# 128 unused bytes per partition ahead of the activation buffers of a two-block transformer kernel

## The chip, the cores and the metric

The kernel runs on one core of a Trainium2 chip. The metric is the device time of one execution in microseconds (us); three executions were timed and their median is taken.

## The reference, cut to what matters

Two transformer blocks are applied to 256 tokens of width 2048, all in float32. The first has forgetting attention and dilated attention, and an expert layer (PEER) whose 16,384 experts are computed densely here and gated; the second has sliding-window attention with sinks, gated linear attention and stick-breaking attention, and a squared-ReLU feed-forward layer. Almost all of the arithmetic is in the matrix products:

```python
proj = xn @ w_in[layer]                 # 2048 x 6160, later 2048 x 5136
h = h + mixed @ w_out[layer]            # 2048 x 2048
q = (xt @ w_query)                      # 2048 x 2048
u = jnp.take(expert_down, ec, axis=0)   # experts: 16384 x 2048 down, 16384 x 2048 up
...
jnp.square(jax.nn.relu(h @ w1)) @ w2    # 2048 x 8192 and 8192 x 2048
```

## The kernel before

**The product.** Every weight matrix is streamed through SBUF once, in chunks of 256 rows by 512 columns (440 columns in the first input projection, "in1", and 428 in the second, "in2"). SyncE's queue loads a chunk into one of four slots of `raw` (line 420). ScalarE makes a rounded float32r copy `w_hi` (line 585) and VectorE the remainder `w_lo = raw - w_hi` (line 590). The activations are kept transposed, split in the same way: `x_hi` and `x_lo` hold the input of a layer, `a_hi` and `a_lo` the hidden values, each 16 x 256 float32r columns, 16,384 bytes, in each of 128 partitions.

A chunk is two row tiles of 128 (`kk`), for two tiles of 128 tokens (`t`), in three products, hence twelve matmuls:

```python
wh = w_hi[:, c % RING, kk * n:kk * n + n]
wl = w_lo[:, c % RING, kk * n:kk * n + n]
xh, xl = hi[:, k, t * P:t * P + P], lo[:, k, t * P:t * P + P]
mm(o, xh, wh, start=(k == 0), stop=False)
mm(o, xh, wl, start=False, stop=False)
last = mm(o, xl, wh, start=False, stop=(k == KT - 1))
```

The first operand of `mm` behind the output, a tile of activations, is the stationary one: a LDWEIGHTS (engine PEld in the profile) reads 128 columns of it, which are 512 bytes of each partition, and the MATMUL then streams the 512, 440 or 428 columns of weights. The lines are 1674 to 1676 in `chunk` (expert layer and feed-forward layer) and 1831 to 1833 in `part` (everything else). Every matmul has a LDWEIGHTS of its own.

**The order.** TensorE's instructions are written out in one order, with `Fori` loops over the like rounds of the expert and feed-forward layers. Between the chunks stand the small matmuls of the attention, and transposes: `pe.transpose(out, in_, ident)` loads `in_` as the stationary operand and streams the identity from `fix`. The transposes that the prediction speaks of are those of the spilled hidden values (`hid_ring`, line 1950), of the residual `h` and of `mix` (line 2016); the sums of the gates of the linear attention (line 2051) load 96 columns of `g_log` and stream 2 columns of `kc`:

```python
for hh in range(GLA_H):
    for t in range(NT):
        at = 4 * hh + 2 * t
        last = mm(ps[0:GLA_K, 4, at:at + 2], g_log[:, t, GLA_K * hh:GLA_K * (hh + 1)], KC(K_HALF, 2),
                  start=True, stop=True)
```

**The memory.** `sb(name, shape, dt, stack)` allocates SBUF in the order of the calls, each tensor at the next multiple of 32 bytes. In order stand `raw`, `w_hi`, `w_lo`, `h`, `fix`, `ident_b`, `back`, a few small ones, `big` (73,856 bytes, in which `proj1`, `proj2`, `mix`, `g_log`, `hid_ring`, `sc` and others are views), and then the four activation buffers. Tensors that are alive while some of the activation buffers are not lie over the same addresses: `srch`, `kc1`, `mask_b`, `c_parts`, `zero`, `pick`, `junk`, `kc`, `sinks`, `nsink`, `gw`, `blT`, `k_end`, `bias_t` and `biased`. In the layout before, `x_hi` begins at byte 163,200 of a partition, which is 318 x 512 + 384. The starts by their remainder at division by 512 are: `raw`, `w_hi`, `w_lo`, `h` and `fix` 128; `big` 256; `x_hi`, `x_lo`, `a_hi`, `a_lo`, `srch`, `kc1`, `kc` and `zero` 384.

Of the kernel before, what the change touches and what calls it, by code (L numbers as in the profile page):

```python
# [26 lines left out]
P = 128  # L27
# [137 lines left out]
def build(nc, a, out):  # L165

    ctx = ExitStack()
    with ctx:
        def sb(name, shape, dt=F32, stack=ctx):
            return stack.enter_context(nc.sbuf_tensor(name, shape, dt))  # L170
# [59 lines left out]
        grow2 = back_flat[0:64, 0:128]  # L230

        with ExitStack() as part:
            x_hi = sb("x_hi", [P, KT, S], F32R, part)
            x_lo = sb("x_lo", [P, KT, S], F32R, part)
            a_hi = sb("a_hi", [P, KT, S], F32R, part)
            a_lo = sb("a_lo", [P, KT, S], F32R, part)
# [2038 lines left out]
```

How the kernel before makes its waits and increments, by code:

```python
        @block.sync  # L413
# [1 line left out]
            def load(B, c, src):  # L415
                q = SUB * B + c
                if not static(q) or q >= RING:
                    sp.wait_ge(lo_made, q - RING + 1)
                n = src.shape[1] * src.shape[2]
                sp.dma_start(raw[:, c % RING, 0:n], src.rearrange("p k n -> p (k n)")).then_inc(raw_loaded[c % RING], 16)
# [28 lines left out]
                phase(False, r, 0)  # L449
            with sp.Fori(0, PEER_ROUNDS) as r:
                phase(True, PEER_ROUNDS, r)
            b0 = sections["in2"][0]
            weights = {"in2": a["w_in_2"], "out2": a["w_out_2"], "mlp": a["w_mlp_in_2"]}
            for s, (name, b, c) in enumerate(SEQ2):
                load(b0 + s // SUB, s % SUB, weights[name][b, c])
            rounds("mlp", 0, MLP_ROUNDS, a["w_mlp_in_2"], a["w_mlp_out_2"])
            for q, t, made, count in ((0, 0, normed_act, 1), (3, 0, normed, 1), (0, 1, normed_act, 2), (3, 1, normed, 2),
                                      (2, 0, normed, 3), (1, 0, normed_act, 3), (2, 1, normed, 4), (1, 1, normed_act, 4)):
                sp.wait_ge(made, count)
                at = slice(q * WIDE, (q + 1) * WIDE)
                sp.dma_start(out[0, t * P:t * P + P, at], h[:, t, at]).then_inc(out_stored, 16)
            sp.wait_ge(out_stored, 16 * NT * NQ)
# [6 lines left out]
            def step(ins):  # L469
                steps[0] += 1
                ins.then_inc(pool_step, 1)
                pool.wait_ge(pool_step, steps[0])
```

## Time and profile before

| | us, where nothing else is said |
|---|---|
| timed executions, median (lowest to highest) | 3091.98 (3090.52 to 3092.07) |
| profiled execution, its own time | 3090.49 |
| its span, from the first to the last instruction | 3088.7 |
| granted TensorE clock over the span, as a share of full speed | 0.999 |
| TensorE matmuls busy | 3061.6 |
| TensorE weight loads busy | 2590.4 |
| VectorE busy | 1779.8 |
| ScalarE busy | 1463.6 |
| GpSimd busy | 633.6 |

The profile is of one execution, whose span leaves 1.8 us of its time outside. A matmul's busy time counts its way through the array too, so that the matmuls of a stream overlap in the records: what a stream costs is read from the distance between two starts, not from the duration of one. "PEld" are the LDWEIGHTS, which run beside the matmul ahead of their own.

### The profile page before, as it was taken

What the parts mean: (1) busy time and instruction counts of PE and PEld (TensorE: products, weight loads), DVE (VectorE), ACT (ScalarE), POOL (GpSimd) and SP (SyncE); (2) the same over time, 40 slices, a digit from 0 to 9 for tenths busy, and PEclk for the clock granted to TensorE, in tenths of its full rate; (3) what the DMA queues carried; (4) which work ended last, traced back from release to release, by engine and by line L of the source; (5) the groups of instructions that cost most, each with busy time, mean ns of one, the idle gap of its engine ahead of it and who ended that gap; (6) DMA issues with size and microseconds to landing.
All of it is one profiled execution on the core that took longest, in us unless ns stands there. A gap on an engine that the chain in (4) does not pass through costs nothing.

```text
span 3088.7 us, 40218 instructions
## 1 busy us (share of the span) xinstructions
PE 3061.6 (99%) x14605; PEld 2590.4 (84%) x14605; DVE 1779.8 (58%) x2360; ACT 1463.6 (47%) x1801; POOL 633.6 (21%) x455
## 2 busy tenths in 40 slices
PE   9999999999999999999999999999999999999998
PEld 8999888888888888888888888899888888888887
DVE  5445564688954444565565556645776454544444
ACT  5445454555544444444444444554565534444453
POOL 3110000188888886000000000000000000000000
PEclk9999999999999999999999999999999999999999
DMA  7764467688888888777777676654445555555554
GB/s 219 245 203 141 146 217 256 187 218 216 217 221 218 218 216 249 271 239 238 238 234 218 217 252 183 188 183 149 134 137 192 190 191 191 188 189 187 192 185 154
DMA packets 217133, 627.70 MB, mean 203 GB/s; under 512 B 58267, under 2 KB 60965, under 8 KB 216624
## 3 DMA queue, kind: packets, MB, share of 16 engines
q1 hardware_dynamic: 157696, 549.79, 57.5%
q0 software_dynamic: 54464, 59.30, 8.0%
q10 hardware_dynamic: 4848, 16.94, 1.4%
q8 instruction: 79, 1.29, 0.2%
q14 instruction: 46, 0.38, 0.0%
HBM read 587.78 MB, written 38.14 MB: 203 GB/s over the span
## 4 chain that ended last, share of the span: by engine, by line
PE 96%; DVE 2%; ACT 1%; issue 0%; DMA 0%; SPq 0%; ACTq 0%; DVEq 0%
PE ps L1676 22%; PE ps L1674 22%; PE ps L1675 22%; PE ps L1831 8%; PE ps L1833 8%; PE ps L1832 8%; PE ps L1950 1%; DVE w_lo L590 1%; PE ps L1780 1%; PE ps L1691 0%; PE ps L1799 0%; PE ps L2016 0%; PE ps L1744 0%; DVE big L1440 0%; PE ps L1819 0%
## 5 line engine op out<-in xcount | busy, mean ns | idle before, releaser
L590 DVE TENSOR_TENSOR w_lo<-raw,w_hi 128x1024 fp32r<-128x1024 f32 (+2 forms) x1072 | 1283.8, 1200 | 1158.4 <-ACT w_hi L585 1155.7
L585 ACT ACTIVATE w_hi<-raw 128x1024 fp32r<-128x1024 f32 (+2 forms) x1072 | 1106.7, 1034 | 1332.9 <-PE ps L1676 1034.6
L1674 PE MATMUL ps<-w_hi,a_hi 128*128 128x512 f32 x1536 | 601.4, 392 | 0.0
L1676 PE MATMUL ps<-w_hi,a_lo 128*128 128x512 f32 x1536 | 598.1, 389 | 0.0
L1675 PE MATMUL ps<-w_lo,a_hi 128*128 128x512 f32 x1536 | 597.8, 389 | 0.0
L1674 PE MATMUL ps<-w_hi,x_hi 128*128 128x512 f32 x1504 | 587.3, 390 | 0.0
L1676 PE MATMUL ps<-w_hi,x_lo 128*128 128x512 f32 x1504 | 585.4, 389 | 0.0
L1675 PE MATMUL ps<-w_lo,x_hi 128*128 128x512 f32 x1504 | 585.2, 389 | 0.0
L487 POOL DMA_INDIRECT gates<-srch x256 | 514.8, 2011 | 157.7 <-issue 79.4
L1831 PE MATMUL ps<-w_hi,x_hi 128*128 128x440 f32 (+2 forms) x1184 | 449.2, 379 | 2.8 <-DVE x_lo L1098 2.7
L1833 PE MATMUL ps<-w_hi,x_lo 128*128 128x440 f32 (+2 forms) x1184 | 437.2, 369 | 0.0
L1832 PE MATMUL ps<-w_lo,x_hi 128*128 128x440 f32 (+2 forms) x1184 | 437.1, 369 | 0.0
L1676 PEld LDWEIGHTS ps<-w_hi,a_lo 128*128 128x128 f32 x1536 | 288.3, 188 | 60.1
L1675 PEld LDWEIGHTS ps<-w_lo,a_hi 128*128 128x128 f32 x1536 | 288.5, 188 | 58.7
L1674 PEld LDWEIGHTS ps<-w_hi,a_hi 128*128 128x128 f32 x1536 | 288.4, 188 | 58.4
L1676 PEld LDWEIGHTS ps<-w_hi,x_lo 128*128 128x128 f32 x1504 | 282.3, 188 | 58.9
L1675 PEld LDWEIGHTS ps<-w_lo,x_hi 128*128 128x128 f32 x1504 | 282.4, 188 | 57.9
L1674 PEld LDWEIGHTS ps<-w_hi,x_hi 128*128 128x128 f32 x1504 | 282.4, 188 | 57.9
L1831 PEld LDWEIGHTS ps<-w_hi,x_hi 128*128 128x128 f32 x1184 | 223.0, 188 | 29.8 <-issue 5.2
L1833 PEld LDWEIGHTS ps<-w_hi,x_lo 128*128 128x128 f32 x1184 | 222.7, 188 | 22.3
L1832 PEld LDWEIGHTS ps<-w_lo,x_hi 128*128 128x128 f32 x1184 | 223.4, 189 | 20.2
L549 POOL DMA_DIRECT2D big<-hid_rows x32 | 17.7, 554 | 472.0 <-PE ps L1950 468.6
(333 smaller groups left out, 1664.5 us busy)
## 6 DMA issues: line engine op xcount, KB each, us to landing
raw<-in_peer_down SPq DMA_DIRECT2D x256, 512.0 KB
raw<-in_peer_up SPq DMA_DIRECT2D x256, 512.0 KB
raw<-in_w_mlp_in SPq DMA_DIRECT2D x128, 512.0 KB
raw<-in_w_mlp_out SPq DMA_DIRECT2D x128, 512.0 KB
raw<-in_w_in SPq DMA_DIRECT2D x112, 440.0 KB
raw<-in_w_in SPq DMA_DIRECT2D x96, 428.0 KB
raw<-in_w_out SPq DMA_DIRECT2D x64, 512.0 KB
gates<-zero POOLq DMA_DIRECT2D x32, 512.0 KB, 5.1
```

What stands on the lines that cost most here:

```text
L487: nc.gpsimd.indirect_dma_start(tables[t], bass.IndirectOffsetOnAxis(ap=slot_at[:, t, slot:slot + 1].bitcast(U32), axis=0), slot_gate[:, t, ...
L549: pool.dma_start(hid_ring[:, buf].rearrange("p t n -> p (t n)"), hid_rows[n]).then_inc(reloaded[buf], 16)
L585: act.activation(w_hi[:, c % RING, 0:2 * n], raw[:, c % RING, 0:2 * n], ACT.Copy).then_inc(hi_made, 1)
L590: nc.vector.tensor_tensor(w_lo[:, c % RING, 0:2 * n], raw[:, c % RING, 0:2 * n], w_hi[:, c % RING, 0:2 * n].bitcast(F32), ALU.subtract).th ...
L1674: mm(o, xh, wh, start=(k == 0), stop=False)
L1675: mm(o, xh, wl, start=False, stop=False)
L1676: last = mm(o, xl, wh, start=False, stop=(k == KT - 1))
L1780: mm(ps[:, 6 + j, at:at + w], qkT[at_, t * P:t * P + P], qkT[at_, S:S + w], start=True, stop=False)
L1831: mm(o, xh, wh, start=(c == first and kk == 0), stop=False)
L1832: mm(o, xh, wl, start=False, stop=False)
L1833: last = mm(o, xl, wh, start=False, stop=(c == last_c and kk == 1))
L1950: last = pe.transpose(ps[:, 4 + 2 * (g % 2) + jj // 2, (jj % 2) * S + t * P:(jj % 2) * S + t * P + P], hid_ring[:, g, t, jj * P:jj * P + P ...
```

## The change

An unused tensor of 32 float32 per partition, 128 bytes, is allocated just ahead of the four activation buffers. It is written and read by nothing. No instruction is added, removed or moved. All tensors that are allocated behind it stand 128 bytes higher: the activation buffers and what shares their addresses.

```diff
@@ -230,6 +230,7 @@
         grow2 = back_flat[0:64, 0:128]

+        sb("to_512", [P, 32])
         with ExitStack() as part:
             x_hi = sb("x_hi", [P, KT, S], F32R, part)
             x_lo = sb("x_lo", [P, KT, S], F32R, part)
```

## Rows read from the trace of the kernel before

**Rows 1.** Page, parts 1 and 2: busy time; granted TensorE clock in 40 slices.

```profile
PE 3061.6 (99%) x14605; PEld 2590.4 (84%) x14605; DVE 1779.8 (58%) x2360; ACT 1463.6 (47%) x1801; POOL 633.6 (21%) x455
...
PEclk9999999999999999999999999999999999999999
```

**Rows 2.** Waits of TensorE: total us, times, longest.

```profile
PE ps L1744 <- DMA h<-in_x: 4.6, 1, 4.6
...
PE ps L1831 <- DVE x_lo L1098: 2.7, 3, 1.3
...
PE ps L2100 <- DVE big L1537: 0.2, 1, 0.2
```

**Rows 3.** Groups of instructions, shapes apart: count, busy us, mean ns, idle before.

```profile
L1674 PE MATMUL ps<-w_hi,a_hi 128*128 128x512 f32 x1536 | 601.4, 392 | 0.0
...
L1674 PE MATMUL ps<-w_hi,x_hi 128*128 128x512 f32 x1504 | 587.3, 390 | 0.0
...
L1674 PEld LDWEIGHTS ps<-w_hi,a_hi 128*128 128x128 f32 x1536 | 288.4, 188 | 58.4
...
L1831 PE MATMUL ps<-w_hi,x_hi 128*128 128x440 f32 x448 | 167.5, 374 | 2.8 <-DVE x_lo L1098 2.7
...
L1831 PE MATMUL ps<-w_hi,x_hi 128*128 128x428 f32 x384 | 141.6, 369 | 0.0
L1831 PE MATMUL ps<-w_hi,x_hi 128*128 128x512 f32 x352 | 140.1, 398 | 0.0
...
L1831 PE MATMUL ps<-w_hi,a_hi 128*128 128x512 f32 x64 | 26.0, 406 | 0.0
```

**Rows 4.** Timeline of TensorE, expert layer: start us, duration us; 24 matmuls apart.

```profile
1000.20 0.39 PE L1675 MATMUL ps<-w_lo,x_hi 128*128 128x512 f32 x1
...
1005.64 0.39 PE L1675 MATMUL ps<-w_lo,x_hi 128*128 128x512 f32 x1
```

**Rows 5.** The same of the first input projection, 24 matmuls apart.

```profile
104.33 0.36 PE L1832 MATMUL ps<-w_lo,x_hi 128*128 128x440 f32 x1
...
109.13 0.36 PE L1832 MATMUL ps<-w_lo,x_hi 128*128 128x440 f32 x1
```

**Rows 6.** The same of the second input projection, 20 matmuls apart.

```profile
2003.95 0.36 PE L1831 MATMUL ps<-w_hi,x_hi 128*128 128x428 f32 x1
...
2007.86 0.36 PE L1833 MATMUL ps<-w_hi,x_lo 128*128 128x428 f32 x1
```

**Rows 7.** Weight loads of line 2051, timeline in three short windows, loads merged.

```profile
2085.82 0.25 PEld L2051 LDWEIGHTS ps<-kc,big 128*96 128x96 f32 x2
...
2086.16 0.25 PEld L2051 LDWEIGHTS ps<-kc,big 128*96 128x96 f32 x2
...
2086.50 0.25 PEld L2051 LDWEIGHTS ps<-kc,big 128*96 128x96 f32 x2
```

**Rows 8.** Line 2051, all its loads: ns lowest/median/highest, first and last start.

```profile
L2051 PEld LDWEIGHTS ps<-kc,big x16: 161/165/166, 2085.4 to 2086.8; 128*96 128x96 f32 x16
```

**Rows 9.** Weight loads of transposes, lines 1950 and 2016, same columns.

```profile
L1950 PEld LDWEIGHTS ps<-fix,big x256: 137/141/142, 1231.0 to 1885.3; 128*128 128x128 f32 x128
...
L2016 PEld LDWEIGHTS ps<-fix,h x64: 138/139/142, 1915.3 to 2377.6; 128*128 128x128 f32 x64
...
L2016 PEld LDWEIGHTS ps<-fix,big x32: 138/141/143, 2243.2 to 2338.4; 128*128 128x128 f32 x32
```

**Rows 10.** Timeline of TensorE, eight transposes of line 1950, merged.

```profile
1503.10 1.04 PE L1950 MATMUL ps<-fix,big 128*128 128x128 f32 x8
```

**Rows 11.** Busy us of each engine from 700 to 800 us.

```profile
700.00:800.00 100.00, 100.00 (x443) 82.81 (x442) 90.59 (x228) 53.78 (x56) 84.10 (x43) 1.00 0.86 220
```

**Rows 12.** Two groups of VectorE's search, shapes apart, columns as in rows 3.

```profile
L1272 DVE FIND_INDEX8 srch<-srch 128x8 uint32<-128x128 f32 x32 | 9.1, 285 | 0.0
L1269 DVE FIND_INDEX8 srch<-srch,big 128x8 uint32<-128x128 f32 x32 | 9.1, 285 | 0.0
```

**Rows 13.** DMA issues: size, median us from issue to landing.

```profile
gates<-zero POOLq DMA_DIRECT2D x32, 512.0 KB, 5.1
```

## The prediction

> **What bounds the kernel now.** I read the page first, parts 1 and 2: TensorE's matmuls are busy for 3061.6 of 3088.7 us, no other engine for more than 58% of it, and the granted clock is at its top digit, 2.4 GHz, in all forty slices [rows 1]. Then the waits of TensorE: nine rows in all, the longest 4.6 us for the first input, and together 15.9 us [rows 2]. So there is no stall worth removing; only the pace of the matmuls themselves can move the time by much. Third, the groups with shapes kept apart, for the counts: the first product of each three stands there 1536 + 1504 + 352 + 64 = 3456 times with 512 columns, 448 times with 440 and 384 times with 428, and each has two sisters, so 10,368, 1344 and 1152 matmuls, 12,864 together [rows 3]. Every one of them reads its stationary tile from the four buffers that the change moves.
>
> Last, the timelines, for the pace, since the durations overlap. With 512 columns, 24 steps take 5.44 us, 0.2267 us each [rows 4]; with 440, 24 steps take 4.80 us, 0.2000 us each [rows 5]; with 428, 20 steps take 3.91 us, 0.1955 us each [rows 6]. The three streams make 10,368 x 0.2267 + 1344 x 0.2000 + 1152 x 0.1955 = 2350 + 269 + 225 = 2844 us. The columns alone, one in each cycle of 2.4 GHz, would take 213.3, 183.3 and 178.3 ns. What is left over is 13.4, 16.7 and 17.2 ns for each matmul, in sum 139 + 22 + 20 = 181 us. That remainder is the only place in which a large gain could lie, and the question of this case is whether it hangs on where the stationary tile begins.
>
> **The change part by part.** It adds no instruction, wait or transfer, and it moves none past another. The sum has therefore only terms for instructions whose operand begins elsewhere.
>
> *The weight loads of the main stream.* Each reads 128 columns of 4 bytes, 512 bytes of a partition. They begin at remainder 384 now, since every tile is a whole multiple of 512 bytes into its buffer, and so each crosses a 512-byte boundary; afterwards they begin at 0 and cross none. No load of the main stream begins at 0 in the trace of before, so I look for others. Line 2051 is the nearest. `g_log` begins 41,088 bytes into `big`, which gives 256 + 128 = 384; each next `hh` is 384 bytes further, so its four groups begin at 384, 256, 128 and 0, and each `t` is 1536 bytes, no change. The profile shows each of the eight products as two loads (16 for eight calls), four for one `hh`. A load of 96 columns is 384 bytes long: from 0 and from 128 it stays inside its 512 bytes, from 256 and from 384 it crosses. It streams only two columns, so here the loads set the pace, and any difference between loads would be seen in full. The second group starts at 2085.82, the third at 2086.16, the fourth at 2086.50 us [rows 7]: 0.34 us for four loads of the second group (crossing) and 0.34 us for four of the third (not crossing), 85 ns a load. The durations of all sixteen lie between 161 and 166 ns, with the median at 165 [rows 8]. The remainder 0 shows nothing of its own, and crossing costs nothing.
>
> The transposes say the same with 128 columns, a full 512 bytes: from `hid_ring` (16,384 bytes into `big`, remainder 256) the median load is 141 ns, from `h` (128) 139, from `mix` (49,280 bytes into `big`, 384) 141 [rows 9]. These two groups of rows bound a change of the load itself at about 2 ns either way.
>
> *What hides it.* In the stream a load runs beside the matmul ahead of its own: 188 ns of 227 [rows 3, 4]. Its duration holds waiting and latency; what it needs of the engine is shown where loads set the pace. Eight transposes take 1.04 us with the last one's own 0.272 us, so (1.04 - 0.272) / 7 = 110 ns each [rows 10]; line 2051 scaled from 96 to 128 columns is 85 x 128 / 96 = 113 ns [rows 7]. Against a matmul of 227, 200 or 195.5 ns there are at least 80 ns of cover. A load that became 2 ns cheaper or dearer changes no step. If that cover were gone, or if the 2 ns went into the remainder behind each matmul, it would be 2 x 12,864 = 26 us.
>
> *The moving operand, and its distance from the stationary one.* `w_hi` and `w_lo` stay at remainder 128. If reads of the two operands got in each other's way by where they begin, the distance between them would matter, and the change takes it from 384 - 128 = 256 to 0 - 128, that is 384. The trace has other distances already: the second half of a chunk (`kk` = 1) begins 1760 bytes on with 440 columns, at remainder 352, a distance of 32; with 428 columns 1712 bytes on, at 304, a distance of 80. Twelve matmuls hold six of each half, and in all 24 steps of the first and 20 of the second projection the printed step is 0.20 and 0.19 to 0.20 us, with no alternation in sixes [rows 5, 6]. A difference is thus under the 10 ns of a printed row for one step, and under 10 / 6, some 2 ns, over a half chunk. This gives the same two ends, -2 and +2 ns for each matmul, and I take 0, the value of every row above.
>
> The Trainium skill, page "SBUF — State Buffer", section "Specifications (TRN2)", gives SBUF lines of 16 bytes, and a penalty for each access that goes to a new line. Remainders 384 and 0 are both multiples of 16, so a tile touches the same number of lines before and after, and by that rule the change is worth nothing; the loads of line 2051 agree, with 165 ns throughout [rows 8]. The page "TensorE: Matmul & The Clock Gate", section "Back-to-back issue gap", gives N / 2.4 + 2.5 ns for matmuls by themselves, 215.8 ns for 512 columns, 11 ns below the step of 227 ns here [rows 4]; no page lays such a difference on the start of the stationary operand, and with that figure in every 512-column step the time would come out, as an estimate from the page, 10,368 x 10.9 = 113 us lower.
>
> *The instructions that share the moved addresses.* ScalarE and VectorE write the activation buffers, and TensorE waits for such a write for 2.7 us in one row and under that in the others [rows 2]. VectorE's search works in `srch`, which goes from 384 to 0, and there is the thinnest cover outside TensorE: VectorE is busy for 90.59 us of the 100 from 700 to 800 us [rows 11]. The same FIND_INDEX8 reads `sc` in `big` (256) in one group and `srch` (384) in the other, and both take 285 ns [rows 12], so I cost the move at 0; 2 ns for each of 228 instructions in these 100 us would be 0.5 us against 9.4 us of cover. The DMAs from `zero` and into `kc1`, `kc` and `bias_t` begin at other remainders; the 32 from `zero` take 5.1 us to land [rows 13], are issued by GpSimd, and no transfer but that of the input stands in the waits of TensorE [rows 2]. 0 us.
>
> **The sum.** 3090.49 us, the profiled execution's own time, plus nothing. The runs shown lie up to 1.6 us above it, with the median at 3091.98. A repeated measurement should fall among them; I take their middle, 3091.5 us.
>
> **The rivals.** *Boundary (faster).* The remainder of 13 to 17 ns behind each matmul is caused, wholly or in part, by float32r loads that cross a 512-byte boundary while a matmul streams. For it speaks that all 12,864 cross and all have the remainder, and that the rows for remainder 0 are of plain float32 with two columns streaming. Against it: crossing costs nothing where loads are alone and would be seen best [rows 7, 8], and the cover of 80 ns lies between. Its price at the full remainder is 181 us, 2911 us; at the 2 ns of the bound, 3066 us. It decides from 0.5 ns a matmul, 6.4 us.
>
> *Distance (slower).* With stationary and moving operand at a distance of 384 in place of 256, reads of the two meet more often. No row has just this distance, and the spread of the half chunks leaves room for 2 ns: 26 us, 3117 us. It decides from the same 0.5 ns. Against it stand three distances (256, 32, 80) without a difference that the rows show.
>
> *VectorE falls behind (slower, a smaller case).* Only from 600 to 900 us is it near full; it would have to lose more than 9.4 us in 100, 41 ns for each of 228 instructions. A loss of 10% there would cost about nothing, one of 15% some 4 us in each 100, up to 12 us: 3104 us.
>
> *The pad doesn't align the buffers.* If the allocator put them elsewhere, the time would be the same still, by the rows for other remainders; this case is inside the forecast.
>
> **How the numbers follow.** A measurement of this kernel tells about 0.2%, 6.2 us, from no change; over 12,864 matmuls that is 0.48 ns each. I give no change 0.86, with the padding that fails inside it; the boundary 0.08, since the main stream's own kind of load at 0 isn't in the trace; the distance 0.05; VectorE 0.01. So faster 0.08, same 0.86, slower 0.06. The range is the forecast with half a nanosecond a matmul on each side, 12,864 x 0.5 = 6.4 us: 3085.1 to 3097.9. It leaves out the 2 ns ends of both rivals, which together hold less than 2 in 10.
>
> **What would show it right or wrong.** Right: the timelines of the three streams again step by 0.227, 0.200 and 0.195 us; the loads of line 1674 stay at 188 ns; TensorE's busy time stays within 6 us of 3061.6; its waits stay below 20 us. Wrong: a step of 226 or less, or of 228 or more, in the middle of the expert layer; loads of the main stream shorter than 188 ns with a shorter step (if only the load gets shorter, the cover was right); TensorE waiting for `w_lo` between 600 and 900 us. The weakest link is that plain float32 loads stand in for float32r loads under a full stream.

## The result and the profile after

The changed kernel takes 3149.55 us (median; 3147.90 to 3151.17) against 3091.26 us for the kernel before in the same comparison (3090.52 to 3092.07). The ratio is 1.0189, with a 95% interval of 1.0177 to 1.0201: slower by 58 us, where no change was forecast.

The page of the changed kernel, parts 1 and 2 (it answers to [rows 1]), shows that all of it is TensorE: its busy time rises by 59.1 us, its idle time doesn't move (27.1 us before, 27.0 after), and the clock is full. GpSimd is busy for 17.6 us more, but TensorE waits for none of it.

```profile
PE 3120.7 (99%) x14605; PEld 2594.2 (82%) x14605; DVE 1779.9 (57%) x2360; ACT 1464.6 (47%) x1801; POOL 651.2 (21%) x455
...
PEclk9999999999999999999999999999999999999999
```

The waits of TensorE after [rows 2] are as they were, 15.9 us in sum. So nothing is late: the same instructions follow each other more slowly. Three of the nine rows:

```profile
PE ps L1745 <- DMA h<-in_x: 4.9, 2, 4.6
...
PE ps L1832 <- DVE x_lo L1099: 2.7, 3, 1.3
...
PE ps L2101 <- DVE big L1538: 0.2, 1, 0.2
```

The groups of instructions after, with their shapes apart [rows 3] (each line stands one further down), tell which. The matmuls of 512 columns have a mean of 397 and 396 ns for 392 and 390. Those of 440 and 428 columns didn't change, and neither did the weight loads, 188 ns.

```profile
L1675 PE MATMUL ps<-w_hi,a_hi 128*128 128x512 f32 x1536 | 609.5, 397 | 0.0
...
L1675 PE MATMUL ps<-w_hi,x_hi 128*128 128x512 f32 x1504 | 595.7, 396 | 0.0
...
L1675 PEld LDWEIGHTS ps<-w_hi,a_hi 128*128 128x128 f32 x1536 | 289.3, 188 | 65.8
...
L1832 PE MATMUL ps<-w_hi,x_hi 128*128 128x440 f32 x448 | 167.4, 374 | 2.7 <-DVE x_lo L1099 2.7
L1832 PE MATMUL ps<-w_hi,x_hi 128*128 128x428 f32 x384 | 141.6, 369 | 0.0
```

The timeline of TensorE after, in the expert layer [rows 4], gives the step: 15 matmuls from 1018.91 to 1022.41 us, 0.2333 us each, where it was 0.2267.

```profile
1018.91 0.40 PE L1677 MATMUL ps<-w_hi,x_lo 128*128 128x512 f32 x1
...
1022.41 0.39 PE L1677 MATMUL ps<-w_hi,x_lo 128*128 128x512 f32 x1
```

The loads by themselves are untouched by the move too: line 2052 after is to the nanosecond what line 2051 was [rows 8], though `kc`, its moving operand, went from 384 to 0. These loads stream two columns each, though, and say nothing of a full stream.

```profile
L2052 PEld LDWEIGHTS ps<-kc,big x16: 161/165/166, 2125.9 to 2127.3; 128*96 128x96 f32 x16
```

Summed over all starts in the two traces, the 5568 steps of 512 columns from `x_hi` and `x_lo` take 33.3 us longer (227.0 ns to 233.1 in the mean of the undisturbed ones, those under 250 ns), the 4800 from `a_hi` and `a_lo` 26.2 us (227.0 to 232.5), those of 440 columns 0.6 us longer and those of 428 columns 0.8 us shorter. Together that is 59.3 us, the whole of the difference, and on average 5.7 ns for each of the 10,368 matmuls of 512 columns (6.0 in the first stream, 5.5 in the second).

### The profile page after: what moved, and what is told of

Read it like the earlier page. It is cut to its first block, busy times and chain, and to the rows that moved or that the text cites. A ratio compares the mean times of both kernels' runs of the same rounds, so it can differ in the third digit from the quotient of the medians.

```text
span 3147.7 us, 40218 instructions
## 1 busy us (share of the span) xinstructions
PE 3120.7 (99%) x14605; PEld 2594.2 (82%) x14605; DVE 1779.9 (57%) x2360; ACT 1464.6 (47%) x1801; POOL 651.2 (21%) x455
## 4 chain that ended last, share of the span: by engine, by line
PE 97%; DVE 2%; ACT 1%; issue 0%; DMA 0%; SPq 0%; ACTq 0%; DVEq 0%
PE ps L1677 22%; PE ps L1676 22%; PE ps L1675 22%; PE ps L1832 8%; PE ps L1833 8%; PE ps L1834 8%; PE ps L1951 1%; DVE w_lo L591 1%; PE ps L1781 1%; PE ps L1692 0%; PE ps L1800 0%; PE ps L2017 0%; PE ps L1745 0%; DVE big L1441 0%; PE ps L1819 0%
## 5 line engine op out<-in xcount | busy, mean ns | idle before, releaser
L1675 PE MATMUL ps<-w_hi,a_hi 128*128 128x512 f32 x1536 | 609.5, 397 | 0.0
L1677 PE MATMUL ps<-w_hi,a_lo 128*128 128x512 f32 x1536 | 606.2, 395 | 0.0
L1676 PE MATMUL ps<-w_lo,a_hi 128*128 128x512 f32 x1536 | 606.0, 395 | 0.0
L1675 PE MATMUL ps<-w_hi,x_hi 128*128 128x512 f32 x1504 | 595.7, 396 | 0.0
L1677 PE MATMUL ps<-w_hi,x_lo 128*128 128x512 f32 x1504 | 593.9, 395 | 0.0
L1676 PE MATMUL ps<-w_lo,x_hi 128*128 128x512 f32 x1504 | 593.8, 395 | 0.0
L488 POOL DMA_INDIRECT gates<-srch x256 | 531.9, 2078 | 156.5 <-issue 77.3
```

What stands on the lines that cost most here:

```text
L488: nc.gpsimd.indirect_dma_start(tables[t], bass.IndirectOffsetOnAxis(ap=slot_at[:, t, slot:slot + 1].bitcast(U32), axis=0), slot_gate[:, t, ...
```

## The experiments

Three theories were open. By the **distance theory**, what counts is where the stationary tile begins relative to the moving operand: 384 - 128 = 256 bytes before, 0 - 128, or 384 of 512, after. By the **start theory**, a stationary tile that begins at a multiple of 512 is slow by itself. By a third, TensorE's reads meet those and the writes of other engines or of the DMAs.

**Everything moved by 128.** The unused tensor goes ahead of the first one.

```diff
+        sb("ahead", [P, 32])
         raw = sb("raw", [P, RING, 2 * WIDE])
```

> The 128 unused bytes stand ahead of the first tensor in place of ahead of the activation buffers, so every tensor moves by 128: stationary tiles begin at 0 of 512 as in the changed kernel, the moving operand at 256 in place of 128. Distance theory (what counts is where the stationary tile begins relative to the moving operand, 256 before, 384 in the changed kernel): the distance is again 256, so the time is that of before, 3091 us, within 0.2%, and the 512-column step 227 ns. Start theory (a stationary tile that begins at a multiple of 512 bytes is slow by itself): 3150 us, step 232 to 234 ns.

Measured: 3091.24 us, ratio 0.9999 (0.9990 to 1.0009). The tiles begin at 0 of 512, just as in the changed kernel, and the time is that of before. The start theory has fallen.

**256 unused bytes ahead of the activation buffers** (`[P, 64]` in place of `[P, 32]`).

> 256 unused bytes ahead of the activation buffers: stationary tiles at 128 of 512, moving operand at 128, distance 0. Start theory: no longer a multiple of 512, so 3091 us and 227 ns. Distance theory: a third distance; if reads of the two meet most when they begin alike, it is the slowest of all, over 3150 us; in any case it need not be 3091.

Measured: 3090.51 us, ratio 0.9998 (0.9989 to 1.0008). Distance 0 is as good as distance 256; that the two should be worst where they begin alike was a wrong guess.

**384 unused bytes** (`[P, 96]`).

> 384 unused bytes: stationary tiles at 256 of 512, moving operand at 128, distance 128. Start theory: 3091 us. Distance theory: the distance is 128 where the changed kernel has 384 (that is -128); if only its size counts, 3150 us as the changed kernel, if the sign counts, another time between 3091 and 3200 us.

Measured: 3149.68 us, ratio 1.0190 (1.0173 to 1.0207), the changed kernel's time again. Distances 384 and 128 are alike and so are 256 and 0, as if the distance counted with a period of 256 bytes; the sweep below tries it. Busy time from 900 to 1000 us, expert layer, in three traces: 443 matmuls of 512 columns touch the 100 us with 256 unused bytes,

```profile
900.00:1000.00 100.00, 100.00 (x443) 1.00 0.81 219
```

and 431 with 384:

```profile
900.00:1000.00 100.00, 100.00 (x431) 1.00 0.79 210
```

Ahead of everything, the 128 bytes leave 442:

```profile
900.00:1000.00 100.00, 100.00 (x442) 1.00 0.82 220
```

**A sweep with nothing else running.** A program of its own, with the chunk's order of matmuls:

```python
for m in M_OFFS:                 # moving operand: 0, 32, ... 480 bytes further
    for s in S_OFFS:             # stationary tile: the same
        for _ in range(REPEATS):     # 2 chunks, 24 matmuls
            last = chunk(s, m)
```

> Computes none of the reference: it loads x, makes float32r tiles of it, runs 6144 matmuls of 512 columns in the order of a chunk (x_hi with w_hi, x_hi with w_lo, x_lo with w_hi, two token tiles, two row tiles) and stores x. 24 matmuls for each of 16 x 16 starts of the stationary and of the moving operand, 32 bytes apart, with ScalarE, VectorE and the DMAs idle. Distance theory: the step depends on the difference of the two starts, 227 ns where it is 256 and more at some others, and stays the same along a diagonal. Start theory: it depends on the stationary start alone, more at 0. A third theory, that the price comes from other engines' or the DMAs' reads and writes of SBUF meeting those of TensorE: about 216 to 227 ns at every start, with no pattern, since nothing else runs.

In the 24 matmuls of one pair of starts, the first to the last start is 23 steps. The timeline of TensorE in the sweep, stationary and moving operand both at 256: 770.67 to 775.89 us, 226.9 ns a step by these printed times.

```profile
770.67 0.39 PE L85 MATMUL ps<-w_hi,x_hi 128*128 128x512 f32 x1
...
775.89 0.40 PE L87 MATMUL ps<-w_hi,x_lo 128*128 128x512 f32 x1
```

The same with the stationary tile at 128, 128 bytes from the moving operand: 748.37 to 753.74, 233.5 ns.

```profile
748.37 0.40 PE L85 MATMUL ps<-w_hi,x_hi 128*128 128x512 f32 x1
...
753.74 0.39 PE L87 MATMUL ps<-w_hi,x_lo 128*128 128x512 f32 x1
```

All pairs, worked out in this way from the starts in the trace, in ns (four of the sixteen rows; all cells of one distance modulo 256 agree within 1.4 ns over the sixteen, save for the first pair, which holds the start of the program):

```
stationary at  0   32   64   96  128  160  192  224  256  288  320  352  384  416  448  480
moving 256   228  233  233  234  234  233  229  233  227  233  233  234  234  233  229  233
moving 288   233  228  233  233  234  234  233  229  233  227  233  233  234  234  233  229
moving 320   229  233  227  233  233  234  234  233  229  233  227  233  233  234  234  233
moving 384   233  233  229  233  227  233  233  234  234  233  229  233  227  233  233  234
```

The step is the same along each diagonal and comes again after 256 bytes, and ScalarE, VectorE and the DMAs were idle. The stretch from 700 to 800 us of the sweep shows it (PE, PEld, ScalarE, GpSimd, the clock, the share and the rate of the DMAs; VectorE doesn't stand there, having done nothing):

```profile
700.00:800.00 100.00, 100.00 (x433) 81.00 (x432) 0.00 (x0) 0.00 (x0) 1.00 0.00 0
```

So the distance theory holds, and the third theory has fallen: TensorE alone makes the price.

**Steps of 4 bytes.** Moving operand at a multiple of 512, stationary tile at 64 starts, 48 matmuls each.

> Computes none of the reference, as the sweep before it. 512 columns, moving operand at a multiple of 512 bytes, stationary tile at 64 starts 4 bytes apart, 48 matmuls each. Distance theory with a period of 256 bytes, as the sweep in steps of 32 bytes has it: 227 ns at 0, 233 at 32, 233 at 64, 234 at 96 and 128, 233 at 160, 229 at 192, 233 at 224. If the price hangs on 32-byte pieces, the seven starts between two of these have the value of one of them; if it hangs on finer ones, some start may be under 227 ns, and a kernel faster than both could be built from it. Nothing under 215 ns is expected, since 512 columns alone take 213.3.

Measured, 47 steps each: 226.7 ns at 120, 144, 156, 228 and 252 bytes, 227.7 at 132, and from 228.3 to 237.1 at all others but the first, which holds the program's start. So no theory of 32-byte pieces explains it; neighbours 4 bytes apart differ by up to 7 ns. No start goes below 226.7 ns, which the kernel before has already.

**Other widths.** The same program with fewer moving columns, then with fewer loaded ones.

> Computes none of the reference. First the distances 0 to 224 in steps of 32 bytes with 512, 496, 480, 448, 440, 428, 384 and 256 moving columns, then 512 moving columns with loads of 128, 96, 64 and 32 stationary columns, 48 matmuls each. If reads of the load meet reads of the streaming matmul, the price of a bad distance should shrink with the columns that are loaded: 6 to 7 ns at 128 columns, about half at 64, little at 32. If it is a fixed cost of a matmul's start, it stays at 6 to 7 ns. For 440 and 428 columns the trace of before showed no difference between the halves of a chunk, so at most 2 ns between distances is expected there, against 7 ns at 512; the sum over columns then stays under 7 ns for all narrower ones.

Mean step in ns (45 steps each, the first two left out), by the stationary tile's start:

```
bytes                0     32     64     96    128    160    192    224
512 columns      257.0* 233.4  233.4  234.4  232.6  233.3  228.9  233.3
496              220.0  226.7  220.0  223.4  223.3  224.6  226.8  224.4
480              216.7  213.3  216.0  217.8  220.0  219.8  218.4  220.0
448              206.5  204.4  202.2  200.0  204.0  205.3  200.0  206.7
440              200.0  200.0  200.0  200.0  200.0  200.0  200.0  200.0
428              196.0  193.3  193.3  193.3  200.0  193.3  195.3  193.3
384              173.4  173.3  174.7  176.6  176.0  176.6  173.4  176.6
256              120.0  118.3  117.8  117.3  118.6  119.8  117.8  117.8
512, load of 128 227.4  233.4  233.4  234.4  232.6  233.3  228.9  233.3
512, load of 96  230.0  228.9  228.4  233.3  231.6  231.1  233.3  233.3
512, load of 64  230.2  231.6  232.8  231.4  229.3  231.5  228.4  230.8
512, load of 32  231.7  239.7  231.7  230.6  230.3  233.3  231.8  233.4
* the start of the program
```

Two things. First, 440 columns, the width of most of the evidence in the prediction, is the one width that shows nothing: 200.0 ns at every distance. The timeline at distance 0, 47 steps from 350.57 to 359.97 us,

```profile
350.57 0.36 PE L85 MATMUL ps<-w_hi,x_hi 128*128 128x440 f32 x1
...
359.97 0.36 PE L87 MATMUL ps<-w_hi,x_lo 128*128 128x440 f32 x1
```

and at distance 128, 47 steps from 388.97 to 398.37 us, are alike, 9.40 us each:

```profile
388.97 0.36 PE L85 MATMUL ps<-w_hi,x_hi 128*128 128x440 f32 x1
...
398.37 0.36 PE L87 MATMUL ps<-w_hi,x_lo 128*128 128x440 f32 x1
```

```diff
             x_lo = sb("x_lo", [P, KT, S], F32R, part)
+            sb("to_512", [P, 32], F32, part)
             a_hi = sb("a_hi", [P, KT, S], F32R, part)
...
-            sb("beside", [P, 2 * KT * S], F32, part)
+            sb("beside", [P, 2 * KT * S + 32], F32, part)
```

> Only a_hi and a_lo, and what shares their addresses, move by 128 bytes; x_hi and x_lo stay. Distance theory: 4800 of the 10,368 matmuls of 512 columns get the bad distance, at 5.7 ns each 27 us: 3119 us, with the step of lines 1674 to 1676 at 232 ns for a_hi and a_lo and 227 ns for x_hi and x_lo. A theory in which the place of the neighbours (srch, kc, zero and others, which move too) makes the time: all 58 us or none, with no difference between the two streams.

Measured: 3117.85 us, ratio 1.0084 (1.0070 to 1.0098). In the groups of its trace, only the stream from `a_hi` changed:

```profile
L1675 PE MATMUL ps<-w_hi,a_hi 128*128 128x512 f32 x1536 | 609.4, 397 | 0.0
...
L1675 PE MATMUL ps<-w_hi,x_hi 128*128 128x512 f32 x1504 | 587.3, 390 | 0.0
```

The spans differ by 3116.0 - 3088.7 = 27.3 us, as expected. By the starts in the traces, 25.8 us of it are the 4800 matmuls from `a_hi` and `a_lo`, 5.4 ns each; the 5568 from `x_hi` and `x_lo` take 1269.4 us in both. The last 1.5 us lie with narrower matmuls. `srch`, `kc`, `zero` and the others moved here too, by the same 128 bytes; and the stream from `x_hi` and `x_lo` didn't feel it, so the place of the neighbours is not the cause. The rest of the changed kernel's 59.0 us belongs to the 5568 matmuls that load from `x_hi` and `x_lo`, 33.3 us by the starts.

**Two more pads, to see whether the sweep foretells the kernel.** 192 and 64 unused bytes ahead of the activation buffers (`[P, 48]` and `[P, 16]`).

> 192 unused bytes ahead of the activation buffers: distance 448, which is 192 of 256, with the moving operand where it was. If the sweep by itself tells the kernel's time: 229 in place of 227 ns (228.9 against 226.7), 2.2 ns for 10,368 matmuls, 23 us, so 3114 us. A theory with two values alone, good at multiples of 256 and bad elsewhere: 3150 us.

Measured: 3111.00 us, ratio 1.0064 (1.0047 to 1.0081). 3 us under what the sweep's 2.2 ns gave; the theory with two values has fallen. The undisturbed steps in its trace have a mean of 229.0 ns, the sweep's 228.9; what differs is the step to start from, 227.0 ns in the kernel.

> 64 unused bytes: distance 320, which is 64 of 256. By the sweep 233.4 ns, 6.7 ns more for 10,368 matmuls, 69 us: 3160 us at most, 3150 if the kernel pays as much less than the sweep as it did at 128 bytes (58 us for 7.3 ns, which is 76 us).

Measured: 3158.14 us, ratio 1.0215 (1.0198 to 1.0232), between the two figures. The undisturbed steps are 233.3 to 233.4 ns, the sweep's 233.4 again. The sweep orders the pads rightly in the main: multiples of 256, then 192, then the two others. Those two it can't tell apart, 233.4 ns each over all its cells, where the kernel pays 8.5 us more at 64 than at 128 (3158.14 against 3149.68 us). So at 128, where the kernel's steps are 232.5 and 233.1 ns, it is up to 1 ns too high.

**Each operand placed by itself.** `w_hi` at 0, and 8 x 8 x 8 starts of `x_hi`, `x_lo` and `w_lo`, 32 bytes apart.

> Computes none of the reference. As the sweeps with 512 columns, but x_hi, x_lo and w_lo get starts of their own, eight each 32 bytes apart, with w_hi at 0: 512 placements of 24 matmuls. If a matmul pays for the distance between its own two operands, the third of each three (x_lo with w_hi) is slow where x_lo lies badly and the first two are not touched by it. If it pays for the distance between the moving operand and the tile that is loaded meanwhile for the next matmul, the second of each three (w_lo streams, x_lo is loaded) is. If any placement goes below 226.7 ns in the mean, a kernel faster than before can be made; none is expected to, since no start 4 bytes apart did.

The mean of the last 17 steps of each placement is 226.9 ns in one of the 512 (`x_hi` at 0, `x_lo` at 128, `w_lo` at 160) and 228.6 or more in all others; the placement with all at 0 came first and holds the program's start. Neither expected pattern showed: grouped by the distance of any two of the four operands, for each of the three products or over all, the means lie between 230.8 and 234.0 ns. The distance of `x_hi` from `w_hi` accounts for 13% of the spread, each other one for less than 5%. What the placements do show is that the good distance belongs to the whole stream and not to a matmul: with `w_lo` alone off 0 the steps are 229.6 to 233.6 ns, with `x_lo` alone 230.9 to 233.6, with `x_hi` alone 229.1 to 233.9. Were only the matmuls dearer that have the moved tile as an operand, a moved `w_lo` or `x_lo`, in one product of three, would cost some 2 ns in the mean, which gives about 229 ns. Where `x_hi` and `x_lo` move together the sweep's steps come back (233.2, 233.5, 234.2, 233.1, 233.1, 228.8 and 233.4 ns for 32 to 224 bytes). Which reads meet, if any do, stays open; 24 matmuls after a changed placement may also be too few for some of the mixed placements to settle. Nothing beats the placement of before.

## Why the prediction was wrong

**What bounds the kernel** was read rightly: the pace of the matmuls and nothing else. The step of 226.7 ns was right, and so was the threshold, half a nanosecond a matmul. The change cost 5.7 ns for each matmul of 512 columns.

**The step that failed** is "The moving operand, and its distance from the stationary one". It took the halves of a chunk with 440 and with 428 columns, at distances of 32 and 80, as rows for the distance in general, and carried a bound of 2 ns over to 512 columns. The reading of these rows stands: by the exact starts the two halves of a chunk differ by 0.6 ns at 440 columns and 0.9 at 428 (undisturbed steps, those under 215 ns). What can't be done is to carry it over, as the sweep over widths shows: at 440 columns every distance gives 200.0 ns, at 428 seven of eight lie within 3 ns, at 512 every distance in steps of 32 bytes but 0 and 192 costs 6 to 7. And of the three distances (256 at every width, 32 at 440 and 80 at 428 columns) the 512-column stream itself had only one, 256, the good one. All 10,368 matmuls with 512 columns stood at one distance; the trace held no row for another. The ends of the unknown cost should have come from what the stream can lose, not from rows of another width.

**The weight loads** were costed rightly, at nothing, and the load's duration stayed 188 ns. But **what hides it**, the 80 ns of cover, was no protection, because the price is not that of a slower load. The stream got slower with loads of equal duration. "A load that became 2 ns cheaper or dearer changes no step" answers a question that the change didn't ask, and no run here tests it.

**The sum** was 3090.49 us plus nothing. The missing term is 10,368 x 5.7 ns = 59 us.

**The rivals.** *Distance* is what happened: same condition, same sign, but sized at 2 ns and 3117 us, and given 0.05. The reason that it gives, reads of the two that meet more often, is not shown by any run. Its argument against itself, three distances without a difference, is the failed step again. *Boundary* has fallen: tiles at 0 of 512 that cross nothing run at the pace of before with the weights moved along (3091.24 us), and at 128 of 512, where every load crosses, too (3090.51 us). *VectorE falls behind* didn't come: TensorE's waits are unchanged. Its price was also read too high: before, VectorE is near full from 600 to 800 us alone (89.03 and 90.59 us busy of 100) and has 77.74 us from 800 to 900, so its upper end was some 8 us and not 12.

**The rules cited.** The Trainium skill's 16-byte lines ("SBUF — State Buffer", "Specifications (TRN2)") gave, as the prediction applied them, no change for two starts that are both multiples of 16. The measurement decides against using it in this way: starts 32 bytes apart cost up to 7 ns a matmul. The N / 2.4 + 2.5 ns of the Trainium skill's page "TensorE: Matmul & The Clock Gate", section "Back-to-back issue gap", was reached by none of the placements tried: the least with 512 columns is 226.7 ns, against 215.8.

**The signs named ahead.** The step of 0.2333 us in the expert layer is the "228 or more" that was to prove it wrong. Two signs of being right came all the same, loads of 188 ns and 15.9 us of waits: neither can see this cost.

## What to carry to other kernels

In a kernel that is nothing but a stream of matmuls with a load each, the start addresses of the two operands are a parameter of the stream: keep the difference between stationary and moving start at a multiple of 256 bytes, for all the stationary and moving tensors that the stream mixes, sweep it by itself for the width in use, and check after every new allocation ahead of them that it still holds. A round address by itself is worth nothing; padding one operand and not the other cost 1.9% here. And a row shows the cost of an address only for the width at which it was measured: where all instructions of a kind stand at one placement, their trace can't say what another would cost.

## What the runs showed of the hardware that was not expected

- The step of a 512-column float32r matmul with a load of 128 columns depends on the distance of the two starts with a period of 256 bytes: 227 ns at 0, 229 at 192, 233 to 234 at 32, 64, 96, 128, 160 and 224, with nothing else running. Between these, starts 4 bytes apart differ by up to 7 ns. In the kernel, one whole pad of 128 bytes cost 58 us, and one of 256 nothing.
- The steady steps of many placements fall on multiples of 6.67 ns, 16 cycles of 2.4 GHz: 193.3, 200.0, 213.3, 220.0, 226.7, 233.3. At other placements single steps follow a repeating pattern off this grid (231 to 238 ns at 96 bytes with 512 columns), and with 256 columns most means lie off it too (117.3 to 120.0). A guess, not shown: the step is rounded up to such a grid, so that some widths, 440 among them, have no room for an address to matter. Why there is a grid, no run here shows.
- A load of 32 columns in place of 128 made the 512-column stream no faster, and cost it the good distance (231.7 for 227.4 ns).
- The durations of full loads didn't move with the distance, 188 ns in the median in every run: the price shows only in the distance between two starts. Narrower loads are shorter (161, 135 and 108 ns in the mean for 96, 64 and 32 columns), and the stream behind them is no faster.
